# Expert items of 32 token slots in place of 64, with the down projection in two partial sums

## What is computed

```python
logits = (xt @ w_router + b_router)
top_val, top_idx = lax.top_k(logits, TOP_K)          # 4 of 32 experts for each token
gates = jax.nn.softmax(top_val, axis=-1)
...
gu = xb @ w_gate_up[e] + b_gate_up[e]                # xb: the tokens of expert e, (n, 1024) @ (1024, 2048)
gate, up = jnp.split(gu, 2, axis=-1)
gate = jnp.minimum(gate, SWIGLU_LIMIT)
up = jnp.clip(up, -SWIGLU_LIMIT, SWIGLU_LIMIT)
hmid = (up + 1.0) * (gate * jax.nn.sigmoid(SWIGLU_ALPHA * gate))
out = hmid @ w_down[e] + b_down[e]                   # (n, 1024) @ (1024, 1024)
y[tok] += gate_weight * out
```

```
41 14 37 18 43 23 35 27 23 26 48 34 20 36 38 40 28 25 32 69 16 23 18 29 48 32 52 24 23 38 37 27
```

## Time and profile before

| | us |
|---|---|
| median of 3 runs | 1189.17 (1188.57 to 1190.3) |
| profiled execution, its time | 1188.51 |
| its span | 1186.7 |
| TensorE busy | 1165.0 |
| VectorE busy | 302.4 |
| ScalarE busy | 220.7 |
| moved from HBM | 439.50 MB |

### The profile page before, as it was taken

How to read it: one execution, slowest core, us unless ns; L and a number is a source line. 1 busy time by engine, 2 the same in 40 slices (tenths; PEclk the granted TensorE clock), 3 DMA queues, 4 the chain that set the end, 5 groups by cost and what they waited for, 6 DMA issues and landing times.

```text
span 1186.7 us, 14208 instructions
## 1 busy us (share of the span) xinstructions
PE 1165.0 (98%) x5344; PEld 490.9 (41%) x5344; DVE 302.4 (25%) x698; ACT 220.7 (19%) x446; POOL 18.5 (2%) x17
## 2 busy tenths in 40 slices
PE   9999999999999999999999999999999999999996
PEld 4475556854333333333333333333333333333332
DVE  3366543344511111112111111111111122111112
ACT  2220551312111111111111210211111111111112
POOL 0030010000000000000000000000000000000000
PEclk9999999999999999999999998999999999999998
DMA  9900378359999999999999999999999999999994
GB/s 364 402 1 1 126 284 329 147 220 376 413 428 427 429 434 431 428 435 428 432 427 434 430 431 429 432 431 430 432 429 432 428 435 430 422 428 428 428 423 180
DMA packets 33604, 441.34 MB, mean 372 GB/s; under 512 B 5008, under 2 KB 5264, under 8 KB 16688
## 3 DMA queue, kind: packets, MB, share of 16 engines
q1 hardware_dynamic: 32544, 439.87, 87.9%
q10 hardware_dynamic: 1008, 0.69, 0.2%
HBM read 439.50 MB, written 1.05 MB: 371 GB/s over the span
## 4 chain that ended last, share of the span: by engine, by line
PE 85%; DMA 12%; DVE 1%; issue 0%; ACT 0%; another core or an unknown queue 0%; POOLq 0%; ACTq 0%
PE quad L1620 34%; PE quad L1646 16%; DMA ring<-in_w_gate_up 12%; PE y_banks L1585 5%; PE quad L1569 4%; PE y_banks L1395 2%; PE quad L1196 2%; PE y_banks L1196 2%; PE y_banks L1226 1%; PE quad L1577 1%; PE quad L1595 1%; PE y_banks L1372 1%; PE quad L1380 1%; PE y_banks L1380 1%; PE y_banks L1514 1%; PE quad L1514 1%
## 5 line engine op out<-in xcount | busy, mean ns | idle before, releaser
L1620 PE MATMUL quad<-ring,work 128*64 128x512 f32 x2112 | 466.1, 599 | 8.3 <-DMA ring<-in_w_gate_up 8.3
L1620 PEld LDWEIGHTS quad<-ring,work 128*64 128x64 f32 x2112 | 150.8, 138 | 301.4 <-issue 288.2
L1646 PE MATMUL quad<-ring,work 128*64 128x512 f32 x1056 | 233.9, 594 | 0.0
L1646 PEld LDWEIGHTS quad<-ring,work 128*64 128x64 f32 x1056 | 87.2, 137 | 133.0 <-issue 118.6
L1133 DVE TENSOR_SCALAR work<-quad 128x512 f32<-128x512 f32 x33 | 22.8, 692 | 330.2 <-PE quad L1620 330.2
L669 ACT ACTIVATE work<-work 128x512 f32<-128x512 f32 x33 | 20.8, 630 | 440.7 <-DVE work L1133 440.7
L1585 PE MATMUL y_banks<-work 64*128 64x512 f32 x272 | 67.6, 615 | 0.7 <-ACT work L680 0.7
L1043 DVE CAST work<-cst 96x64 bf16 (+1 forms) x34 | 6.5, 191 | 239.5 <-PE quad L1620 239.5
L1569 PE MATMUL quad<-h,work 128*64 128x512 f32 x272 | 64.2, 592 | 0.0
L678 ACT ACTIVATE work<-quad 128x512 f32<-128x512 f32 x33 | 19.7, 597 | 229.9 <-PE quad L1646 229.9
L669 ACT ACT_TABLE_LOAD x33 | 42.3, 1283 | 1.1 <-issue 0.5
(11 more groups left out here) (275 smaller groups left out, 841.0 us busy)
## 6 DMA issues: line engine op xcount, KB each, us to landing
ring<-in_w_gate_up SPq DMA_DIRECT2D x40, 4096.0 KB, 36.4
ring<-in_w_gate_up SPq DMA_DIRECT2D x41, 2048.0 KB, 22.4
ring<-in_w_down SPq DMA_DIRECT2D x20, 4096.0 KB, 35.4
ring<-in_w_down SPq DMA_DIRECT2D x21, 2048.0 KB, 19.9
ring<-in_w_gate_up SPq DMA_DIRECT2D x28, 512.0 KB, 9.3
ring<-in_w_mkv SPq DMA_DIRECT2D x8, 1024.0 KB, 24.3
ring<-in_w_in SPq DMA_DIRECT2D x7, 976.0 KB, 17.6
ring<-in_w_down SPq DMA_DIRECT2D x12, 512.0 KB, 8.0
```

Of the source, the lines that this page charges most:

```text
L1620: ins = mm(bank[n // 2][lo:lo + BLK, :], xgT[:, k % 4 * P + k // 4 * BLK:k % 4 * P + k // 4 * BLK + BLK], up_rows(j, k)[:, n * 512:(n + 1) ...
L1646: ins = mm(bank[3][n * BLK:(n + 1) * BLK, :], lhs, down_rows(j, f)[:, n * 512:(n + 1) * 512], start=(f == 0), stop=(f == KC - 1))
```

## The change

- The first two experts (LEAD = 2) keep items of WIDE = 64 slots. All others have items of BLK = 32 slots. The number of items has its upper bound at 64 in place of 48, so a fourth block of the item table is computed behind item 0.
- In an item of 32 slots the stationary operand of gate/up has 32 columns. The four blocks of 512 outputs go to the four quarters of bank 0 (`hidden_rows`).
- The down projection of such an item has 32 columns too. Its 8 products go by turns to two sums (even and odd f), so four quarters of bank 3 are filled: two blocks of outputs times two partial sums. The scatter is unchanged in shape: its matrix holds every slot's gate twice, so it adds up the two sums.
- The transposes of gathered and hidden values have 64 rows in place of 128. They are now ordinary products with an identity of 64 x 64 (`turned`), 128 x 64 out.
- Between the two kinds, TensorE closes the wide item's open sums, gathers the first item of expert 2 anew in 32 slots, and VectorE and ScalarE do their parts again.
- How many items an expert has is computed by rounding count/block up, not by comparing with multiples of 64.

```diff
-BLK = 64
-NOVF = SEQ * TOPK // BLK
-NITEM = NE + NOVF
+WIDE, BLK = 64, 32
+NITEM = NE + SEQ * TOPK // BLK
...
-            for lo, n in ((4, 12), (16, 16), (32, 16)):
+            for lo, n in ((4, 12), (16, 16), (32, 16), (48, 16)):
                 item_table(lo, n)
-            with dve.Fori(1, items) as w:
-                whole_item(w)
+            with dve.Fori(1, wide) as w:
+                whole_item(w, WIDE, 0)
+
+            dve.wait_ge(S["gathered"], wide + 1)
+            choose(LEAD, 0, BLK)
+            dve.wait_ge(S["chunks_used"], wide * NCH)
+            choose_bias(LEAD, BLK)
+            gathered_out(wide + 3, BLK)
+            with dve.Fori(wide, items) as w:
+                whole_item(w, BLK, 1)
...
+            def turned(dst, src):
+
+                rows = src.shape[0]
+                if rows == P:
+                    return pe.transpose(dst, src, ident)
+                return mm(dst, src, ident[0:rows, 0:rows], start=True, stop=True)
...
+            def hidden_rows(n, block):
+
+                b, lo = divmod(n * block, P)
+                return bank[b][lo:lo + block, :]
...
-                        lo = n % 2 * BLK
-                        ins = mm(bank[n // 2][lo:lo + BLK, :], xgT[:, k % 4 * P + k // 4 * BLK:k % 4 * P + k // 4 * BLK + BLK],
+                        lo = (k % 4 * 2 + k // 4) * block
+                        ins = mm(hidden_rows(n, block), xgT[:, lo:lo + block],
                                  up_rows(j, k)[:, n * 512:(n + 1) * 512], start=False, stop=(k == KC - 1))
...
-                    lhs = hT[:, f % 4 * P + f // 4 * BLK:f % 4 * P + f // 4 * BLK + BLK]
+                    lhs = hT[:, (f % 4 * 2 + f // 4) * block:(f % 4 * 2 + f // 4 + 1) * block]
+                    sums = P // 2 // block
                     for n in range(2):
-                        ins = mm(bank[3][n * BLK:(n + 1) * BLK, :], lhs,
-                                 down_rows(j, f)[:, n * 512:(n + 1) * 512], start=(f == 0), stop=(f == KC - 1))
+                        lo = n * (P // 2) + f % sums * block
+                        ins = mm(bank[3][lo:lo + block, :], lhs,
+                                 down_rows(j, f)[:, n * 512:(n + 1) * 512], start=(f < sums), stop=(f >= KC - sums))
...
-            for e in range(1, NE):
+            for e in range(1, LEAD):
+                with pe.Fori(end_of(e - 1), end_of(e)) as w:
+                    item(w, e * NCH, WIDE, 0)
+
+            for n in range(4):
+
+                mm(hidden_rows(n, WIDE), up_bf[0:96, 0:WIDE], bgu[0:96, n * 512:(n + 1) * 512], start=False, stop=True)
+            wide = end_of(LEAD - 1)
+            pe.wait_ge(S["gsel_ready"], wide + 1)
+            pe.wait_ge(S["pick_ready"], wide * TT + 2 * TT)
+            gather(BLK)
+            biases(wide + 2, BLK)
+            gathered_columns(wide + 3, BLK)
+            for e in range(LEAD, NE):
                 if e == NE // 2:
                     down_biases()
                 with pe.Fori(end_of(e - 1), end_of(e)) as w:
-                    item(w, e * NCH)
+                    item(w, e * NCH, BLK, 1)
```

More of the change, by code:

```diff
@@ L1069, in _ @@
             link(dve.tensor_tensor(place_e, spl(bank[3][:, 0:2 * NE], 2), unset, ALU.add))
[L1070 to L1075, removed]
+            choose(0, 0, WIDE)
+            choose_bias(0, WIDE)
+            for lo, hi, block in ((0, LEAD, WIDE), (LEAD, NE, BLK)):
+                link(dve.tensor_scalar(extra[:, lo:hi], bank[3][:, 64 + lo:64 + hi], 1.0 / block, -0.5 - 0.5 / block,
+                                       ALU.mult, ALU.add))
+            link(dve.tensor_scalar(extra, extra, magic, None, ALU.add))
+            link(dve.tensor_scalar(extra, extra, -magic, 0.0, ALU.add, ALU.max))
             link(dve.tensor_reduce(total_f, extra, X, ALU.add))
@@ L1142, in whole_item @@
[L1142 to L1146 removed]
+                dve.tensor_tensor(hid, up, sig, ALU.mult).then_inc(S["hmid_ready"], 1)
+            def whole_item(w, block, regathered):
+                choose_next(w, block, regathered)
+                activated(w, block)
+                gathered_out(w + (3 + regathered), block)
+                place_gates(w, block)
             item_table(0, 4)
@@ L1560, in _, with gather @@
             mm(bank[3][:, 64:96], ones_bf[:, :], mask_bf[:, 1, :], start=False, stop=True).then_inc(S["rank_mm"], 1)
-            def gather(first=False):
+            def turned(dst, src):
[3 more added lines that the diff above has]
+                return mm(dst, src, ident[0:rows, 0:rows], start=True, stop=True)
+            def gather(block, first=False):
                 for t in range(TT):
@@ L1606, in quarter_in, with item @@
                     pe.wait_ge(ld_tail[j][q], 32)
-            def item(w, j):
-                pe.wait_ge(S["xg_ready"], w + 1)
+            def item(w, j, block, regathered):
+                pe.wait_ge(S["xg_ready"], w + (1 + 2 * regathered))
                 for k in range(KC):
-                    if k == 2:
+                    if k == 2 and not regathered:
                         pe.wait_ge(S["xg_ready"], w + 2)
@@ L1661, in _ @@
             residual_in(1, 1)
-            gather(first=True)
+            gather(WIDE, first=True)
             pe.wait_ge(S["counts_ready"], 1)
             first = pe.value_load(first_i[0:1, :], min_val=1, max_val=NITEM - 1)
-            biases(0)
+            biases(1, WIDE)
             for i in range(2):
@@ L1676, in _ @@
             with pe.Fori(0, first) as w:
-                item(w, 0)
+                item(w, 0, WIDE, 0)
             def down_biases():
```

143 lines of the change are left out of this document (79 added, 64 removed).

## The result

The changed kernel takes **1212.55 us** (median of 4 runs, 1211.23 to 1213.78) against 1188.87 for the kernel before (4 runs on the same chip): a ratio of 1.02, 95% interval 1.0188 to 1.0212. The forecast was 1216 us. The profiled execution has a span of 1210.7 us against 1186.7, 24.0 more, with 11.4 us of it behind the last item, as before.

The account below looks back on a forecast made before the run. TensorE (98% busy) and the weight stream were both full, the stream slower per expert. Last item's end 1175.3 becomes 1201.5 plus 1 us clock loss: +27 on 1188.51 gives 1215.5, forecast 1216 us (+2.3%), range 1204 to 1290.

Parts of the forecast that it names:

- Four tiles side by side: 32-slot items: four 32-column tiles overlap without loss, gate/up taking 6.94 us instead of 13.88, down projection 3.54 instead of 7.07.
- The step from one tile to two was nearly free: Gate/up matmuls: two 64-column tiles run 1.98 times as fast as one; reason for choosing the lower end for four tiles.
- The empty queue: Load queue during expert 2's first item: empty from 346.7 to 361.3, expert 4's first 2 MB landing at 368.5, 17 us later.
- The tail: After expert 29's last up chunk lands at 1118: 1.74 us of up part, 10.6 of that item, four more items, 70.2.
- VectorE's chain and the changeover: Experts 1 and 2: expert 1's item waits 2.3 us for VectorE's picks, changeover costs 5.0 us, expert 2 starts at 342.0.
- Waits for gate/up weights: Runs of one-item experts: TensorE starves, 17.55 us an item against 29.4 of stream, with 84 us of waits in sum.
- With loads hidden that is 0.86 for a group of eight, with loads exposed 1.29: Sixteen 64-row transposes per 32-slot item, two groups of eight: 1.29 us taken for each, within an item of 17.55 us.
- with hidden loads 16.7: 32-slot item's total: the lower alternative, 16.7 us if the transposes' loads are hidden, against the chosen 17.55.
- 1200.6: End of the last item in us, from expert 29's landing at 1118 plus TensorE's work behind it; 1175.3 before the change.
- the 1 us for clock: Experts just ahead of the end: 1 us lost to a lower clock after waits, added to 1201.5.
- Three tiles and two tiles: Rivals on overlap: only three tiles, item 21.0 us, 1291 (chance 0.13); none beyond two, item 28 us, about 1592 (0.07).
- the rival that needs 445: Not slower: the stream speeds up when TensorE reads less; 445 GB/s gives no change, 450 gives 6 us faster; chance 0.08.

Follow-up runs that it names:

- late_refill: The kernel before, all 64-slot items, with expert 4's first load waiting for expert 2's last chunk instead of its first: 1205.23 us, ratio 1.0138.
- one_item_e2: The changed kernel with expert 2 given one 32-slot item instead of two, its tokens from the 33rd on left out: 1197.04 us, ratio 1.007.
- nwide8: The changed kernel with the first eight experts in 64-slot items instead of the first two, nothing left out: 1196.64 us, ratio 1.0066.
- one_item_e30: The changed kernel with expert 30 given one item instead of two, its tokens from the 33rd on left out: 1204.13 us, ratio 1.0124.
- last_narrow_3: The changed kernel with only the last expert in 32 slots, and without the fourth block of the item table: 1186.53 us, ratio 0.9978.
- one_item_each: The changed kernel with every expert from 2 on given one 32-slot item, tokens from the 33rd on left out: 1188.03 us, ratio 0.9994.
- one_item_e13: The changed kernel with expert 13 given one 32-slot item instead of two, its tokens from the 33rd on left out: 1211.91 us, ratio 1.0194.
- last_narrow: The changed kernel with all experts in 64-slot items except expert 31, which has 32 slots: 1186.12 us, ratio 0.9976 to the kernel before.
- one_sum: The changed kernel with one sum instead of two partial sums in the down projection of 32-slot items: 1265.81 us, ratio 1.0652.

## Why the prediction was right

- **Four tiles side by side.** 7.00 and 3.64 us, taken as 6.94 and 3.54. "The step from one tile to two was nearly free" carried over to four: 64 instructions that take 64 x 429 = 27.5 us alone ran in 7.00, 3.9 times. "TensorE: Matmul & The Clock Gate" of the Trainium skill, Part 3, with its 2.38 for three column tiles and 3.07 for four row tiles, does not describe this; the measurement decides.
- **The empty queue.** The forecast had it from 346.7 to 361.3 with the load landing at 368.5; it landed at 368.4. late_refill shows that this alone costs 16.5 of the 24.0 us, one_item_e2 that closing it gives back 15.6. What the forecast didn't have is the second hole, at expert 19, 1.9 us of stream. The reading of the token list has a slip without effect: expert 2 has 37 tokens and not 43, which are expert 4's; either needs two items.
- **The tail.** Expert 29's last up chunk was put at 1118 and landed at 1119.0. That the four items behind it are TensorE's own, with the experts of two items among them, nwide8 and one_item_e30 show: 5.7 us stay in nwide8 beyond what its stream is late, and 8.2 go with one of these items.
- **VectorE's chain and the changeover.** The gather of expert 1 starts at 324.83 (forecast 324.3), expert 2 at 342.61 (342.0).
- **Waits for gate/up weights: right by luck.** They sum to 83.5 us, and the forecast had 84. But the 44 items are 0.82 us shorter each than forecast, 36 us in all, and with the stream setting the pace that would be 36 us more of waiting. It isn't, since the items behind the waits run at a lower granted clock (32 up instructions take 5.2 us from 501.8 on and 6.5 from 550.4, where half of 7.00 would be 3.5; the clock was 0.83 in 500:510 and 0.67 in 550:560). From 342.6 to 1199.4 there are 856.8 us; 44 items of 16.73, the 3.6 of the down biases and the 85.2 of waits for loads leave 32 that no wait explains. The forecast had put next to nothing there (1 us, in the tail). Two misses of 36 and 32 us cancelled. Up to the last wait neither reached the time, which the stream sets.
- **What was mis-sized** is the term "With loads hidden that is 0.86 for a group of eight, with loads exposed 1.29 ... I take 1.29, twice". Sixteen of the products that transpose took 1.73 us, 108 ns each, so their loads are hidden. With the copy (0.37 for 0.48) the item is 16.73 us and not 17.55. The other end of the sum ("with hidden loads 16.7") stood in the forecast and was not chosen, because of how a row was read: 4.21 us for eight K=32 products (526 ns each) was taken for exposed loads. The loads of those products, in the kernel before (start us, us, count, idle before), say otherwise:

```profile
710.09 0.18 PEld L1684 LDWEIGHTS y_banks<-work 32*128 32x128 f32 x1 [0.24 <-issue]
710.52 0.18 PEld L1684 LDWEIGHTS y_banks<-work 32*128 32x128 f32 x1 [0.24 <-issue]
...
711.81 0.18 PEld L1684 LDWEIGHTS y_banks<-work 32*128 32x128 f32 x1 [0.24 <-issue]
712.24 0.18 PEld L1684 LDWEIGHTS y_banks<-work 32*128 32x128 f32 x1 [0.24 <-issue]
```

And windows of the same stretch (columns as in the earlier trace rows):

```profile
712.00:713.00 1.00, 1.00 (x3) 0.18 (x1) 0.00 (x0) 0.00 (x0) 0.00 (x0) 0.77 1.07 459
713.00:714.00 1.00, 1.00 (x3) 0.24 (x4) 0.00 (x0) 0.00 (x0) 0.00 (x0) 0.50 0.99 426
```

They come every 0.43 us to the last one at 712.24, the full-clock pace of a 512-column product; the excess lies behind them, where the granted clock goes to 0.50. The 0.64 of the earlier trace rows had stood beside the row, and the two were read as two facts.

- **How this adds up.** From 1200.6: the landing is 1.0 later, the quarter and the gather behind the wait cost 1.9 more at a lower clock (3.36 + 1.97 for 1.74 + 1.72), and five items are 0.82 shorter, which takes off 4.1: 1199.4, as measured. I had taken 1201.5 + 1. So the 1 us for clock was 1.9, and the item's error of 4.1 outweighed it.
- **The rivals.** Three tiles and two tiles fall by the 7.00. The items that waited for nothing held a granted clock of 1.00 (342 to 500 and 1131 to 1199.4 us); below 1 it was only in and behind the waits for loads. The GB/s line of the changed kernel doesn't pass 433. "DMA: Bandwidth & Descriptors" of the Trainium skill, under "Where 436 GB/s comes from", puts the ceiling of a core's 16 ports at 435 GB/s. The trace agrees, with 435 as the highest slice of the earlier trace rows, and by that rule the rival that needs 445 had no room. The same section lets the memory's side, some 358 GB/s, bind such loads; the 422 to 435 of the earlier trace rows, from the twelfth slice to the last but one, contradict that, and the measurement decides.

What stays open: why the stream ends 1.1 us later in last_narrow_3 and 2.1 in one_item_each. Much of it is there early: by 400 us they have moved 110.22 and 109.73 MB against 110.49 before, 0.6 and 1.8 us of stream. What held them back, no run here shows.

## What to carry to other kernels

When TensorE and the weight stream are both full, ask of every edit *when it frees a buffer*, and not only how much time it takes: here 58 us less TensorE time made the kernel 24 us slower, since a ring two experts deep was released once per expert, and a second item put that release 17 us later on a queue that ran dry. A hole in a stream that is full to the end was not made up in any run here, and a gain on the other engine in the middle was worth next to nothing (0.8 of 16.7 us at expert 13). When a forecast matches, check its parts too: the waits matched here because two misses cancelled. What is worth shortening is the work behind the last load: one expert in 32 slots gave 0.24%, thirty of them cost 2%.

## What the runs showed of the hardware

- Four 32-column f32 tiles side by side sustain 109 ns for an instruction of 512 moving columns (64 in 7.00 us), against 217 for two of 64 columns and 429 for the full array.
- 64-row products on one row tile, with a load of 128 columns before each, ran at 108 ns with 64 moving columns: the loads were hidden. By the rows of the kernel before, the columns are 54 ns (429 x 64/512) and the load is 107 (1.71/16 in the earlier trace rows); one behind the other they would take 161.
- The granted clock fell without a wait. The same eight K=32 products, each time between the two transposes of an item's gates and the next up part (items of 64 slots in four of the profiles, of 32 in ten), took 3.62 or 3.63 us in eight of the fourteen profiles of this study, 3.82 and 3.88 in two, and 4.11 to 4.21 in four (the kernel before, one_item_e13, last_narrow, one_item_each). In the kernel before the granted clock goes to 0.50 between 712.4 and 712.6 while TensorE is busy throughout; its last wait, of 2.5 us, ended at 689.9. last_narrow and last_narrow_3 run the same sequence there, and so do the kernel before and late_refill; in each pair one has it and the other not. What decides, no run here tells.
- The wait of 2.4 us for VectorE's picks in expert 1 left the clock alone in the changed kernel and in six others, and halved it behind the wait in three (last_narrow, one_sum, one_item_e30). The chain of last_narrow, where gather and scatter behind that wait take 5.5 us in place of 3.86:

```profile
324.09 2.86 PE quad L1607 x8
326.95 2.64 PE y_banks L1624 x8
```
